# Two pairs of weight buffers that begin at other bytes of their stores

## What is computed

```python
for l in range(DEPTH):                       # first block
    mod = c_act @ w_ada[l] + b_ada[l]
    h = rms_norm(x, norm_mix[l]) * (1.0 + sc1) + sh1
    proj = h @ w_in[l]                       # 1024 x 7440
    ...                                      # gated delta rule, sliding-window attention
    y_a = o_dn @ w_dn_out[l]
    y_b = swa @ w_swa_out[l]
    x = x + gt1 * (merged @ w_o[l])
    h = rms_norm(x, norm_ffn[l]) * (1.0 + sc2) + sh2
    up_act, up_lin = jnp.split(h @ w_up[l], 2, axis=-1)
    x = x + gt2 * ((jax.nn.silu(up_act) * up_lin) @ w_down[l])
for l in range(DEPTH):                       # second block
    x = x + 0.5 * swiglu(rmsnorm(x, ffn1_norm[l]), ...)
    x = x + hybrid_mixer(...)                # h @ w_in, sparse attention, mLSTM, @ w_out
    x = x + 0.5 * swiglu(rmsnorm(x, ffn2_norm[l]), ...)
```

## Time and profile before

| what | before |
|---|---|
| median of three runs | 2228.66 us |
| time of the profiled execution | 2228.63 us |
| its span, first to last instruction | 2226.8 us |
| TensorE busy | 2145.2 us, 96% |
| VectorE busy | 1505.3 us, 68% |
| ScalarE busy | 1077.0 us, 48% |
| GpSimd busy | 580.9 us, 26% |
| DMA over the span | 172 GB/s mean |
| mean granted TensorE clock | 0.992 |

### The profile page before, as it was taken

The page is one execution under the profiler, slowest core; times in us unless marked ns, Lnnn a source line. Parts: engine busy times, 40 slices in busy tenths (PEclk is TensorE's granted clock), DMA queues, the critical chain, the costliest instruction groups (busy, mean ns, idle before and its releaser), DMA issues.

```text
span 2226.8 us, 39796 instructions
## 1 busy us (share of the span) xinstructions
PE 2145.2 (96%) x17221; PEld 2043.7 (92%) x17221; DVE 1505.3 (68%) x1850; ACT 1077.0 (48%) x1432; POOL 580.9 (26%) x280
## 2 busy tenths in 40 slices
PE   7999999999999999999999999989999999999999
PEld 4988899899998888989999999879999999879999
DVE  6967775787678766667666556876556556786555
ACT  3666573433356647443445435554445444555333
POOL 0963324899248260475000000100000000100000
PEclk9999999999999999999999999999999999999999
DMA  9752336677656315566555555335555555434553
GB/s 320 236 170 81 108 121 198 225 252 239 205 181 216 96 41 168 171 213 205 188 184 176 186 184 166 110 96 189 189 188 172 189 184 177 133 95 149 182 185 129
DMA packets 332856, 383.93 MB, mean 172 GB/s; under 512 B 12551, under 2 KB 315402, under 8 KB 332554
## 3 DMA queue, kind: packets, MB, share of 16 engines
q1 hardware_dynamic: 332234, 381.23, 53.6%
q10 hardware_dynamic: 448, 0.16, 0.0%
HBM read 380.32 MB, written 1.05 MB: 171 GB/s over the span
## 4 chain that ended last, share of the span: by engine, by line
PE 75%; DVE 15%; ACT 7%; issue 3%; DMA 0%; SPq 0%; ACTq 0%; DVEq 0%
PE bank L753 16%; PE bank L754 15%; PE bank L755 15%; DVE weights_low L1441 6%; PE bank L993 5%; PE bank L992 5%; PE bank L991 5%; ACT weights_high L2178 4%; DVE arena L1569 2%; PE bank L769 1%; PE bank L892 1%; PE bank L1210 1%; PE bank L1225 1%; PE bank L884 1%; PE bank L1047 1%
## 5 line engine op out<-in xcount | busy, mean ns | idle before, releaser
L1441 DVE TENSOR_TENSOR weights_low<-ring,weights_high 128x2048 fp32r<-128x2048 f32 (+1 forms) x304 | 759.2, 2497 | 431.6 <-ACT weights_high L2178 431.0
L753 PE MATMUL bank<-h_high,weights_high 128*128 128x256 f32 x3296 | 937.9, 285 | 23.7 <-DVE weights_low L1441 14.3
L755 PE MATMUL bank<-h_high,weights_low 128*128 128x256 f32 x3296 | 925.8, 281 | 0.0
L754 PE MATMUL bank<-h_low,weights_high 128*128 128x256 f32 x3296 | 923.0, 280 | 0.0
L2178 ACT ACTIVATE weights_high<-ring 128x2048 fp32r<-128x2048 f32 (+1 forms) x304 | 582.2, 1915 | 693.3 <-PE bank L755 537.1
L753 PEld LDWEIGHTS bank<-h_high,weights_high 128*128 128x128 f32 x3296 | 622.0, 189 | 43.4 <-DVE weights_low L1441 23.8
L754 PEld LDWEIGHTS bank<-h_low,weights_high 128*128 128x128 f32 x3296 | 620.6, 188 | 3.4 <-issue 3.3
L755 PEld LDWEIGHTS bank<-h_high,weights_low 128*128 128x128 f32 x3296 | 620.3, 188 | 0.0
L991 PE MATMUL bank<-hidden_high,weights_high 128*128 128x256 f32 x1056 | 295.3, 280 | 1.4 <-DVE hidden_low L1707 0.9
L993 PE MATMUL bank<-hidden_high,weights_low 128*128 128x256 f32 x1056 | 296.2, 281 | 0.0
L992 PE MATMUL bank<-hidden_low,weights_high 128*128 128x256 f32 x1056 | 295.2, 280 | 0.0
(11 more groups left out here) (439 smaller groups left out, 2817.7 us busy)
## 6 DMA issues: line engine op xcount, KB each, us to landing
ring<-in_w_in SPq DMA_DIRECT2D x80, 1024.0 KB, 5.3
ring<-in_w_up SPq DMA_DIRECT2D x44, 1024.0 KB, 5.3
ring<-in_ffn_w_gate SPq DMA_DIRECT2D x44, 1024.0 KB, 5.4
ring<-in_ffn_w_up SPq DMA_DIRECT2D x44, 1024.0 KB, 5.4
ring<-in_ffn_w_down SPq DMA_DIRECT2D x44, 1024.0 KB, 5.0
side<-in_w_ada SPq DMA_DIRECT2D x42, 1024.0 KB, 7.8
ring<-in_w_down SPq DMA_DIRECT2D x22, 1024.0 KB, 5.0
ring<-in_w_dn_out SPq DMA_DIRECT2D x8, 1024.0 KB, 5.2
```

The lines of the kernel that those rows point to most:

```text
L753: mm(o[:, m, :], a_, high[:, t, :], start=(t == 0), stop=False)
L754: mm(o[:, m, :], a_, low[:, t, :], start=False, stop=False)
L755: last = mm(o[:, m, :], b_, high[:, t, :], start=False, stop=(t == KT - 1))
L1441: v.tensor_tensor(low, wide(q), high.bitcast(F32), ALU.subtract).then_inc(chunk_split, 1)
```

## The change

The view of a half that holds a 256-column chunk (or a chunk of the second feed-forward matrix) began 12 numbers, 48 bytes, into its store for all four halves. Now those of pair 0 begin 24 numbers, 96 bytes, in, and those of pair 1 begin 56 numbers, 224 bytes, in. The view that holds a 272-column chunk stays at 48 bytes.

```diff
         half_stores = [rounded(n, 14336 + (SLOT + 16) * i, SLOT + 16) for i, n in enumerate(half_names)]
-        shifts = (12, 12, 12, 12)
-        half = lambda i, n: half_stores[i][:, shifts[i]:shifts[i] + KT * n].rearrange("p (t n) -> p t n", t=KT)
-        WH, WL = ([half(2 * i + low, T) for i in range(2)] for low in range(2))
-        wide_high, wide_low = ([half(2 * i + low, WIDE) for i in range(2)] for low in range(2))
+        PLACE_OF = (24, 56)
+        half = lambda i, at, n: half_stores[i][:, at:at + KT * n].rearrange("p (t n) -> p t n", t=KT)
+        WH, WL = ([half(2 * i + low, PLACE_OF[i], T) for i in range(2)] for low in range(2))
+        wide_high, wide_low = ([half(2 * i + low, 12, WIDE) for i in range(2)] for low in range(2))
```

## The result

The changed kernel is slower. Its median is 2233.8 us (2231.59 to 2238.09, 8 runs) against 2227.89 us (2223.82 to 2230.64, 8 runs) for the kernel before: a ratio of 1.003, with a 95% interval from 1.002 to 1.0041. That is 5.9 us more, where 2219 us was forecast. Part of the scatter goes with the mean granted clock (of 100 runs of the kernel before, taken beside the experiments, 17 had 0.993 or more and a median of 2224.3 us, the others 2228.8 us; of the changed kernel's eight, five had that and 2233.6 us, three less and 2235.5 us), so that like against like the change costs some 7 to 9 us.

The account below looks back on a forecast made before the run. The matmul step on PE was taken to bound the kernel. With split and moving-operand uses at 0, a step 0.8 ns shorter at 11.6 us a ns gave 2228.63 less 9.3, forecast 2219 us; range 2196 to 2238, forecast's own 2211 to 2224.

Parts of the forecast that it names:

- What bounds the kernel: Whole kernel: PE busy 96% of the span; matmuls of linear3 and second feed-forward matrix 61% of chain, hardly waiting for weights.
- The price of a nanosecond: 13,824 matmuls whose stationary tile moves, 0.84 of a step change reaching the end: 11.6 us per ns of mean step.
- The split costs nothing: Rounding and subtraction on the moved halves: medians stay 1916 and 2293 ns, cost taken as 0.
- The windows no longer alternate: Consecutive chunks around 1300 us, before 5.66 and 5.62 us by turns, would all take about 5.60 us.
- the phase modulo 256: Stationary halves' start bytes modulo 256 decide the matmul step; if windows still alternate, this isn't what decides.
- The lower bound: Weighted sums by line 1028, 111.9 ns each: a load that size goes no faster; 5.6 ns under the mean, 65 us.
- the much faster rival: Load and stream no longer meet at all: 2164 us at the 111.9 ns bound, 2196 half-way; chance 0.13.
- the third part: Stationary loads of the moved halves: mean step falls from 117.5 to 116.7 ns, worth 9.3 us.
- it is slower: Rival: load and moving stream meet in a bad rhythm in both pairs, at most 29 us, 2257.6 us; chance 0.21.
- the row of the chunk at 120.0 ns: One pair 0 chunk, 45 steps from 513.07 to 518.47 us: 2.5 ns over the mean, 29 us if all were alike.
- The rule of the page "SBUF — State Buffer": TensorE never waits at SBUF, with separate read ports for moving operand and weights: change worth nothing, time stays 2228.6 us.

Follow-up runs that it names:

- The second trace: The changed kernel executed once more with nothing altered, to see another execution's chunks; measured in one run: 2234.23 us.

## Why the prediction was wrong, point by point

**What bounds the kernel** stood: the step of the three-fold products is what the change reached, by its place alone, and no wait took the place of the loss.

**The price of a nanosecond** stood. It was put at 11.6 us, from 13,824 matmuls; with those of lines 731 to 733, which the count leaves out, 14,208 have a moved stationary tile, which changes little. Over the 19 traces (this study's kernels but the one with the moving tile turned by itself) a straight line through mean step and time of the profiled execution has a slope of 10.2 us a ns, and the standard deviation of the points about it is 1.8 us. The traces differ also in how long TensorE ran at 1.2 GHz (granted clock 0.50), from 20 to 39 us, and with this time as a second variable the slope is 11.7 us a ns, with a standard error of 0.9. The 0.44 ns by which the changed kernel's trace is slower (117.90 less 117.46) is 4.5 to 5.2 us by the two slopes, where the two executions are 3.0 us apart and the medians 5.9; the changed kernel's trace had 27 us at 1.2 GHz and that of the kernel before 37. The second trace, at 118.14, is 0.68 ns and 5.6 us over the kernel before.

The kernel before lies 2.4 us over the line and the one with both pairs at 48 lies 3.0 us under it; that is why the latter gained 8 us where its steps explain 3. Most of these 5 us can be placed. The time between chunks, over one step each, is 7.5 us in the kernel before for the 16 chunks that start from 479 to 572 us, and 3.7 us in the one at 48 and in the one without shift; the 17 other traces have 6.6 to 8.1. GpSimd is busy for 78.51 of the 80 us from 480 us on in the kernel before, and the subtraction is longer there than its median of 2293 ns. It has a median of 3335 ns in the kernel before (first line) and of 2822 ns with both pairs at 48 (second line):

```profile
L1441 DVE TENSOR_TENSOR weights_low<-ring,weights_high x13: 2292/3335/4462, 480.5 to 556.0; 128x2048 fp32r<-128x2048 f32 x13
...
L1441 DVE TENSOR_TENSOR weights_low<-ring,weights_high x14: 2292/2822/3805, 479.5 to 556.0; 128x2048 fp32r<-128x2048 f32 x14
```

So these two kernels gained some 3.8 us in one stretch by less time between chunks and not by a shorter step. Why they did and the others didn't stays open.

**The split costs nothing** stood: medians of 2293 and 1921 ns, with waits within 4 us. Where GpSimd works, around 500 us, no longer wait took anything back either: the time between chunks given above is 7.8 us in the changed kernel and 7.5 before.

**The windows no longer alternate** stood, at 5.68 us and not at the 5.60 foreseen, and so did the phase modulo 256 that was behind it: the two pairs are alike where their places are.

**The lower bound** was misread. The kernel has 8 sums by line 1028, in float32, and each shows as two matmul records of 128 columns; the 111.9 ns are the step between records. With 256 columns line 769, float32 too, takes 221.9 ns a record. The step grows with the columns, so 111.9 isn't the pace of a load with little to stream beside it, and bounds nothing for `float32r`. The forecast's own number didn't rest on it; that of the much faster rival did.

**The failed step** is in the third part, the size and the sign of the new step: "If the new place is about as much better than that of pair 1 as pair 1 is better than pair 0, both pairs go to 117.2 - 0.5 = 116.7 ns". It took two points for a trend. The map shows that there is none: between 48 and 32 bytes the step rises from 117.2 to 119.9. The reason given with it, that multiples of 32 suit a moving tile at a multiple of 32, is refuted by the 119.9 at 32 and the 117.9 at 128. The measured mean was 117.9 to 118.1 ns in the two traces, where 116.7 was forecast, with most chunks at 118.1 to 118.6: at the border of 117.9 where the rival "it is slower" was said to decide.

**That rival** named the place and the sign rightly, a bad rhythm in both pairs at once, and even the row of the chunk at 120.0 ns, which showed that one place can have two rhythms. Its lasting in both pairs came as it said, though not because an average over two places was lost. The two halves of the change, made apart, are 1.0015 and 0.9982. Beside the old pair 0 the new place was the faster one, and it was lost when its partner moved. The prediction had treated the two pairs as independent.

**The rule of the page "SBUF — State Buffer"** of the Trainium skill, in "Who interferes with whom", that TensorE never waits for anyone at SBUF, would have given no change; the sixteen places, from 115.6 to 120.0 ns, don't agree with it as a statement on time. As far as it speaks of other engines, the traces agree for the split: its writes make no difference to the step, as shown above.

**Five versions beat the kernel before** with an interval below 1. The two best are high 48 and low 112 in both pairs (2220.82 us, 0.9965), and no shift at all (2220.59 us, 0.9965); half of their gain is in the stretch around 500 us. The first has the narrower spread, 2 us over five runs, and that place kept nearly all chunks within 117.0 to 117.5 ns beside each of its four partners (176, 48, 0 and 224).

## What to carry to other kernels

In this kernel, which streams one operand while it loads the other for every matmul, the place of the one against the other was worth up to 3.8% of a step (115.6 to 120.0 ns), and two places didn't tell the third. In a kernel like it, measure each place, with the buffers in the arrangement in which they will alternate. Look at the windows of single chunks and not only at the time, since a good median can be a mixture of two rhythms, and prefer a place that has one rhythm to one that is fastest when it is lucky. When two buffers alternate, a change to one is judged beside the other; try the halves of such a change apart.

## What the runs showed of the hardware

- The distance between two `float32r` matmuls with a 128x128 stationary tile and 256 moving columns is from 115.6 to 120.0 ns at a granted clock of 1.00, depending on the first bytes of the stationary halves against the moving tile modulo 256 and on the chunk before.
- The same instructions on the same bytes can keep up to three distinct steps (115.6, 116.8, 120.0 ns), mostly for as long as no wait comes between: 30 chunks of 48 matmuls at 120.0 in one case. It can also change with no wait seen, as from 118.7 to 120.0 with the low halves at 128 and 0.
- Whether ScalarE and VectorE write the other pair's halves meanwhile makes no difference to it (115.56 and 115.56 ns, 119.79 and 119.95).
- Which one is taken depends on the chunk before (115.6 behind one at 128, 119.8 behind one at 176, 115.6 and 117.0 in turn behind one at 48) and, behind a wait, on something that differs from run to run. A program whose buffers all stand at such a place scatters over 24 us, 1.1%, between runs.
- What in the load and the stream meets, and why the period is 256 bytes, no run here shows.
